# Seven block products in another order, with a third temporary for weight sums, and restored activations loaded behind the gate's weights

## The reference

```python
h = rms_norm(x, norm_g) * (1.0 + scale) + shift
u = h @ w_in          # (2048 x 1024) @ (1024 x D_IN)
(m_q, m_k, m_v, m_o, m_z, m_i, m_f, f_q, f_k, f_v, f_z, f_f) = jnp.split(u, SPLIT_IDX, axis=-1)
# m_q, m_k: causal conv of 4 taps + SiLU; f_q, f_k: RMS norm of each head
# m_v, m_o, f_v: values and an output gate, used as they are
# gate (of c @ w_ada) multiplies the layer's output at the very end
```

## Time and profile before

| | us |
|---|---|
| median of three runs | 1598.61 |
| the profiled execution | 1593.53 |
| its span | 1591.7 |
| PE busy in the span | 1471.6 (92%) |
| DVE busy | 997.8 (63%) |
| ACT busy | 645.1 (41%) |
| granted TensorE clock, mean | 0.974 |

### The profile page before, as it was taken

One profiled execution on the slowest core, in us unless ns is written; L12 is line 12 of the kernel. 1 busy time (PEld: TensorE's weight loads), 2 busy tenths in 40 slices (PEclk: granted clock), 3 DMA queues, 4 the chain that ended last, 5 costly groups with the idle time before them and its releaser, 6 DMA issues.

```text
span 1591.7 us, 21613 instructions
## 1 busy us (share of the span) xinstructions
PE 1471.6 (92%) x7673; PEld 1110.9 (70%) x7673; DVE 997.8 (63%) x2194; ACT 645.1 (41%) x1024; POOL 262.8 (17%) x370
## 2 busy tenths in 40 slices
PE   2999899999499998999999899999999997999998
PEld 2678777778388886887777665555555555888886
DVE  5867777762442466356678585766766747676774
ACT  4733544421021222344445566565655644222220
POOL 2034111102100000011111312103111000122221
PEclk8999999999799999999999999999999999999999
DMA  9374556559653422356665634223151047566761
GB/s 345 133 256 159 178 215 229 214 192 262 198 197 113 140 94 84 129 202 212 226 222 192 186 100 133 54 74 125 45 174 49 16 87 241 164 200 176 188 186 68
DMA packets 157291, 256.95 MB, mean 161 GB/s; under 512 B 11165, under 2 KB 94249, under 8 KB 155833
## 3 DMA queue, kind: packets, MB, share of 16 engines
q1 hardware_dynamic: 132304, 166.45, 34.6%
q0 software_dynamic: 24896, 89.31, 15.2%
HBM read 164.11 MB, written 91.62 MB: 161 GB/s over the span
## 4 chain that ended last, share of the span: by engine, by line
PE 61%; DVE 13%; DMA 12%; ACT 5%; issue 5%; SPq 3%; POOL 0%; DVEq 0%; ACTq 0%
PE a_ps_u L1333 13%; PE m_ps_out L2573 10%; PE f_ps_o L2108 8%; PE f_ps_t L2083 7%; DMA w_in_land<-in_w_in 7%; PE f_ps_s L2071 7%; PE a_ps_u L1290 5%; PE a_ps_u L1264 4%; DVE u_copy L956 2%; DMA gate_piece<-in_w_ada 1%; DMA a_ada_rows<-in_w_ada 1%; SPq L2404 1%; DVE u_copy L967 1%; DVE stage L927 1%; DVE gate_piece L982 1%
## 5 line engine op out<-in xcount | busy, mean ns | idle before, releaser
L1333 PE MATMUL a_ps_u<-v_hi,a_h_hi 128*128 128x512 f32 x384 | 152.5, 397 | 30.8 <-ACT stage L1698 18.7
L1333 PE MATMUL a_ps_u<-v_hi,a_h_lo 128*128 128x512 f32 x384 | 151.4, 394 | 0.0
L956 DVE TENSOR_TENSOR u_copy<-a_ps_u,u_copy 128x512 f32<-128x512 f32 x140 | 94.0, 686 | 27.0 <-PE a_ps_u L1290 24.7
L1333 PEld LDWEIGHTS a_ps_u<-v_hi,a_h_hi 128*128 128x128 f32 x384 | 73.6, 192 | 47.9 <-ACT stage L1698 19.1
L2243 ACT ACTIVATE f_probs_t<-f_ps_t 128x512 f32<-128x512 f32 (+1 forms) x128 | 65.3, 549 | 99.4 <-PE f_ps_t L2083 99.4
L1290 PE MATMUL a_ps_u<-a_h_hi,w_late 128*128 128x512 f32 x320 | 103.0, 389 | 0.0
L1290 PE MATMUL a_ps_u<-a_h_hi,w_in_lo 128*128 128x512 f32 x320 | 101.8, 389 | 0.0
L1290 PE MATMUL a_ps_u<-a_h_hi,w_in_hi 128*128 128x512 f32 x320 | 101.8, 389 | 0.0
L2573 PE MATMUL m_ps_out<-m_w_hi,w_in_hi 128*128 128x512 f32 x256 | 85.9, 412 | 2.0 <-DVE m_update L2726 2.0
L1698 ACT ACTIVATE stage<-a_ps_u 128x512 f32<-128x512 f32 x48 | 28.5, 601 | 142.6 <-PE a_ps_u L1333 128.7
L1333 PEld LDWEIGHTS a_ps_u<-v_hi,a_h_lo 128*128 128x128 f32 x384 | 73.5, 191 | 15.6
(11 more groups left out here) (388 smaller groups left out, 3554.5 us busy)
## 6 DMA issues: line engine op xcount, KB each, us to landing
w_in_land<-in_w_in SPq DMA_DIRECT2D x21, 1024.0 KB, 7.9
scratch_arrays<-stage POOLq DMA_DIRECT2D x14, 1024.0 KB, 4.9
scratch_arrays<-stage POOLq DMA_DIRECT2D x20, 512.0 KB, 3.1
w_in_land<-in_w_in SPq DMA_DIRECT2D x40, 256.0 KB, 3.4
scratch_kept<-w_in_lo POOLq DMA_DIRECT2D x18, 512.0 KB, 3.1
w_in_lo<-scratch_kept POOLq DMA_DIRECT2D x18, 512.0 KB, 3.9
scratch_qkT<-stage POOLq DMA_DIRECT2D x16, 512.0 KB, 4.0
scratch_qkT<-u_copy POOLq DMA_DIRECT2D x16, 512.0 KB, 6.9
```

Source lines behind the costliest of these rows:

```text
L956: dve.tensor_add(out, bank_of(s), other).then_inc(added_up, 1)
L1333: ins = pe.matmul(ps_u[:, half, c, :], h[:, k, first:first + P], w, start=(k == 0 and h is h_hi and w is not v_lo[k]), stop=(k == KT - 1 a ...
```

## The change

The change orders the seven products so that the three which read a block of the landed pair as it is come first, uses a third temporary (in the place of the gates' weights, which are done by then), loads a pair's weights when slot 2 and all four sums of the pair before are done, and orders DVE's, ACT's and POOL's work in a period to match. In the value stage the four restores move behind the gate's pieces and between value blocks, the store of unit 0 moves ahead of a wait in the gates' chain, and the last eight value blocks are split before the combinations. The diff is shown with most of its unchanged lines left out and twelve leading blanks removed.

```diff
@@ -120,6 +120,8 @@
 wg_land = lsb("wg_land", [P, KT, 2 * M_HEADS + F_HEADS])
+with nc.sbuf_tensor("a1_third_sum", [P, NB], F32) as third_sum:
+    pass
 w_gates = lsb("w_gates", [P, KT, GATE_ROWS], F32R)
@@ -278,7 +280,7 @@
 ADDS = 7
-KEPT = (1, 2, 3, 6)
+KEPT = (3, 4, 5, 6)
 KEPT_PAIRS = FIRST_PAIRS - 1
@@ -299,8 +301,8 @@
 
-    return [(LOWER, columns(w, 0)), (UPPER, columns(1 - w, 1)), (LOWER, columns(1 - w, 0)), (LOWER, columns(1 - w, 1)),
-            (UPPER, columns(w, 0)), (UPPER, columns(1 - w, 0)), (UPPER, columns(w, 1))][s]
+    return [(LOWER, columns(w, 0)), (UPPER, columns(w, 0)), (UPPER, columns(1 - w, 0)), (UPPER, columns(1 - w, 1)),
+            (LOWER, columns(1 - w, 0)), (LOWER, columns(1 - w, 1)), (UPPER, columns(w, 1))][s]
 
@@ -317,8 +319,9 @@
 sum_a, sum_b = (as_weights(stage[:, 1, WINDOW + i * NB:WINDOW + (i + 1) * NB]) for i in range(2))
-SLOT_SOURCE = [A11, sum_b, sum_a, sum_a, A12, A22, sum_b]
-SUMS_NEEDED = [0, 2, 1, 4, 0, 0, 3]
+sum_c = as_weights(third_sum[:, :])
+SLOT_SOURCE = [A11, A12, A22, sum_b, sum_a, sum_c, sum_b]
+SUMS_NEEDED = [0, 0, 0, 2, 1, 3, 4]
 
@@ -416,7 +419,6 @@
             eng.wait_ge(combined_lo, 4 * HALF_K)
-            eng.wait_ge(kept_moved[KEPT.index(s)], KEPT_PAIRS * 16)
         elif s < 6:
@@ -498,7 +500,8 @@
         elif p != FIRST_PAIRS:
-            sp.wait_ge(slot_lo, built_count(p - 1, 5))
+            sp.wait_ge(slot_lo, built_count(p - 1, 2))
+            sp.wait_ge(sums_ready, 4 * min(p, FIRST_PAIRS + 1))
         sp.dma_start(pair_land, w_view[:, :, bass.ds(tile_column(kind, i), 2 * P)]).then_inc(w_landed[0], 16)
@@ -507,8 +510,7 @@
                 sp.wait_ge(product_done, PRODUCTS * FIRST_PAIRS)
-                for s in (1, 3):
-                    sp.wait_ge(kept_moved[KEPT.index(s)], KEPT_PAIRS * 16)
+                sp.wait_ge(kept_moved[KEPT.index(3)], KEPT_PAIRS * 16)
             for f in range(2):
@@ -533,14 +535,17 @@
         load_pair(p)
-    sp.wait_ge(slot_lo, built_count(FIRST_PAIRS - 1, 5))
+    sp.wait_ge(slot_lo, built_count(FIRST_PAIRS - 1, 2))
+    sp.wait_ge(sums_ready, 4 * FIRST_PAIRS)
     load_values(0, KT + 4)
     sp.wait_ge(product_done, PRODUCTS * FIRST_PAIRS)
-    for b in (2, 3):
+
+    def restore(b, i):
         here = slice((b - 2) * NB, (b - 1) * NB)
         sp.wait_ge(later_moved, 4 * 16)
-        for i, h in enumerate((h_hi, h_lo)):
-            sp.dma_start(h[:, :, b * NB:(b + 1) * NB].bitcast(F32), scratch["later"][i, :, :, here]).then_inc(later_moved, 16)
+        h = (h_hi, h_lo)[i]
+        sp.dma_start(h[:, :, b * NB:(b + 1) * NB].bitcast(F32), scratch["later"][i, :, :, here]).then_inc(later_moved, 16)
+
     load_raw(1)
@@ -552,9 +557,14 @@
     load_raw(0)
-    load_values(20, 24)
+    restore(2, 0)
+    load_values(20, 22)
+    restore(2, 1)
+    load_values(22, 24)
     load_raw(2)
     load_raw(3)
+    restore(3, 0)
+    restore(3, 1)
     load_values(24, 28)
@@ -696,12 +706,12 @@
         if p + 1 < KEPT_PAIRS:
-            keep_slot(p + 1, 1)
-            keep_slot(p + 1, 2)
+            keep_slot(p + 1, 3)
         if p and p - 1 in WORKED:
...
         if p + 1 < KEPT_PAIRS:
-            keep_slot(p + 1, 3)
+            keep_slot(p + 1, 4)
+            keep_slot(p + 1, 5)
         if p and p - 1 in WORKED:
@@ -731,6 +741,7 @@
     pool.dma_start(f_ends[:, :], scratch["f_end"]).then_inc(chain_loaded, 16)
+    store_unit(0)
     wait_step(pool, "m_next_ready")
@@ -738,7 +749,6 @@
     pool.dma_start(neg_before[:, :], as_rows("f_before")).then_inc(chain_loaded, 16)
-    store_unit(0)
     wait_step(pool, "decay_ready")
@@ -915,15 +925,20 @@
                 elif p:
-                    dve.wait_ge(slot_lo, built_count(p - 1, 3))
+                    dve.wait_ge(slot_lo, built_count(p - 1, 4))
             elif i == 1:
...
                     dve.wait_ge(slot_lo, built_count(p - 1, 6))
+            elif i == 2:
+                if p:
+                    dve.wait_ge(slot_lo, built_count(p - 1, 5))
+                else:
+                    dve.wait_ge(gates_taken, TB)
             else:
-                dve.wait_ge(slot_lo, built_count(p, i - 1))
+                dve.wait_ge(slot_lo, built_count(p, 3))
             out, left, right, op = ((sum_a, A21, A22, ALU.add), (sum_b, sum_a, A11, ALU.subtract),
-                                    (sum_b, A12, sum_b, ALU.subtract), (sum_a, A11, A21, ALU.subtract))[i]
+                                    (sum_c, A11, A21, ALU.subtract), (sum_b, A12, sum_b, ALU.subtract))[i]
             dve.tensor_tensor(out=out, in0=left, in1=right, op=op).then_inc(sums_ready, 1)
@@ -941,17 +956,17 @@
 
-        s = [1, 3, 2, 2, 4, 5, 6][i]
-        out, other = [(u_block(p, 0, 1), u_block(p, 0, 0)), (u_block(p, 1, 0), u_block(p, 0, 1)),
-                      (u_block(p, 1, 1), u_block(p, 1, 0)), (u_block(p, 0, 1), u_block(p, 0, 1)),
-                      (u_block(p, 0, 0), u_block(p, 0, 0)), (u_block(p, 1, 0), u_block(p, 1, 0)),
+        s = [3, 1, 5, 4, 4, 2, 6][i]
+        out, other = [(u_block(p, 0, 1), u_block(p, 0, 0)), (u_block(p, 0, 0), u_block(p, 0, 0)),
+                      (u_block(p, 1, 0), u_block(p, 0, 1)), (u_block(p, 1, 1), u_block(p, 1, 0)),
+                      (u_block(p, 0, 1), u_block(p, 0, 1)), (u_block(p, 1, 0), u_block(p, 1, 0)),
                       (u_block(p, 0, 1), u_block(p, 0, 1))][i]
...
             dve.wait_ge(x_taken, p + 1)
-        elif i != 4:
-            dve.wait_ge(added_up, ADDS * p + [0, 1, 2, 1, 0, 3, 4][i])
-        if i == 1:
+        else:
+            dve.wait_ge(added_up, ADDS * p + [0, 1, 1, 3, 3, 4, 5][i])
+        if i == 2:
             wait_u(dve, p, 1)
@@ -1043,38 +1058,35 @@
             first_step(prev, turns(prev)[0])
-        add_up(p, 0)
         if build is not None:
-            sums(build, (0, 1))
+            sums(build, (0, 1, 2))
             low_slot(build, 0)
             low_slot(build, 1)
-            sums(build, (2,))
         if worked:
             first_step(prev, turns(prev)[1])
-        for i in (1, 2, 3):
-            add_up(p, i)
+        if build is not None:
+            low_slot(build, 2)
+        add_up(p, 0)
+        add_up(p, 1)
         if worked:
...
         if build is not None:
-            low_slot(build, 2)
+            low_slot(build, 3)
             sums(build, (3,))
-        add_up(p, 4)
+        elif p == FIRST_PAIRS - 1:
+            for k in range(4):
+                split_value(k)
         if worked:
...
         if build is not None:
-            low_slot(build, 3)
-        elif p == FIRST_PAIRS - 1:
-            for k in range(4):
-                split_value(k)
-        add_up(p, 5)
+            low_slot(build, 4)
+        for i in (2, 3, 4, 5):
+            add_up(p, i)
+        if build is not None:
+            low_slot(build, 5)
         if worked:
             second_step(prev, turns(prev)[1])
-        if build is not None:
-            low_slot(build, 4)
-        if worked:
             third_step(prev, turns(prev)[1])
-        if build is not None:
-            low_slot(build, 5)
 
@@ -1162,16 +1174,14 @@
     low_combined(0, 2)
-    sums(0, (0, 1))
+    sums(0, (0, 1, 2))
     plain(2)
     low_combined(0, 3)
-    low_slot(0, 0)
-    low_slot(0, 1)
-    sums(0, (2,))
-    low_slot(0, 2)
+    for s in range(4):
+        low_slot(0, s)
     sums(0, (3,))
     plain(3)
-    for s in range(3, 6):
+    for s in (4, 5):
         low_slot(0, s)
@@ -1210,22 +1220,19 @@
         differences(k)
-    split_values(32, 36)
+    split_values(32, PIECES_OF_V)
     for k in (0, 1):
...
         differences(k)
-    split_values(36, PIECES_OF_V)
     for k in (2, 3):
         low_combined(1, k)
-    sums(FIRST_PAIRS, (0, 1))
-    low_slot(FIRST_PAIRS, 0)
-    low_slot(FIRST_PAIRS, 1)
-    sums(FIRST_PAIRS, (2,))
-    low_slot(FIRST_PAIRS, 2)
+    sums(FIRST_PAIRS, (0, 1, 2))
+    for s in range(4):
+        low_slot(FIRST_PAIRS, s)
     sums(FIRST_PAIRS, (3,))
-    for s in range(3, 6):
+    for s in (4, 5):
         low_slot(FIRST_PAIRS, s)
@@ -1274,16 +1281,16 @@
             pe.wait_ge(finished, {0: 3, 2: 4, 4: 2}[s])
-        if p == 0 and s == 1:
+        if p == 0 and s == 2:
             pe.wait_ge(combined_lo, 2 * HALF_K)
...
         elif s == 6:
-            pe.wait_ge(added_up, ADDS * p + 2)
+            pe.wait_ge(added_up, ADDS * p + 1)
         elif p:
-            pe.wait_ge(added_up, ADDS * (p - 1) + {1: 1, 2: 4, 3: 7, 4: 5, 5: 6}[s])
+            pe.wait_ge(added_up, ADDS * (p - 1) + {1: 2, 2: 6, 3: 7, 4: 5, 5: 3}[s])
         rows, cols = operand(w, s)
@@ -1517,7 +1524,7 @@
             return
-        if s in (0, 4, 5):
+        if s < 3:
             act.wait_ge(w_landed[0], (2 + p + 1) * 16)
@@ -1632,20 +1639,22 @@
             first_step(prev, second)
+        if build is not None:
+            high_slot(build, 2)
         if worked:
...
         if build is not None:
-            high_slot(build, 2)
+            high_slot(build, 3)
         if worked:
```

(8 more changed lines are left out.)

## The result

The changed kernel takes 1544.16 us, the median of four runs (1542.01 to 1544.65), against 1598.53 for the kernel before, run beside it. The ratio is 0.9655, with a 95% interval of 0.9638 to 0.9671: 54.4 us less. The forecast was 1542.8, range 1531 to 1562.

The account below looks back on a forecast made before the run. TensorE was taken as the bound. Gains of 12.1 (window one), 37.0 (value stage) and 6.7 (window two) sum to 55.8 us: profiled 1593.5 to 1537.7, plus 5.1 to the median, 1542.8 us; range 1531 to 1562.

Parts of the forecast that it names:

- The ceiling: Both windows and value stage: TensorE loses 70.2 us to waits and low clock, the most this change can gain.
- Window one: First window's block products: earlier loads end VectorE's waits but the first; 4.6 us lost in place of 16.7, gain 12.1.
- the 2.8 us wait: First period of window one: TensorE's wait before product 6 shrinks from 4.8 to 2.8 us, with 1.5 of low clock.
- The gain that it implied: Window one: at the skill page's 4.4 us per load the last wait would go, gain some 4 us larger.
- The value stage: Value stage between the windows: its waits go with their low clock, 37.0 of 37.8 us gained, 0.8 stays.
- the 18.7, 4.7 and 6.6 us: Value stage: TensorE's three old waits, two blamed on restores ahead of gate weights, one on late splits; all to go.
- at 5.2 us each: Value stage: seven gate sums follow the first, made at 17 us, at 5.2 us each, ending at 55.
- rival 1: Value stage: unit 2's store, beside queued restores, makes ScalarE late; 2 us wait, up to 2 of clock; 1545 to 1548; chance 0.15.
- Window two: Second window: three pairs lose about 1.9 us each in place of 4.3, last tile waits 3.2; net gain 6.7.
- Rival 2: Both windows: VectorE becomes the bound, squares 1.4 us late in every NORM pair, window two gains nothing; 1555; chance 0.15.
- Rival 3: Value stage: restores land too late for the second half of tokens, wanted at 125 us; slower, about 1605; chance 0.03.
- Rival 4: Window one: the load starts no earlier in effect, so the window gains only 2 us; 1553; chance 0.07.

Follow-up runs that it names:

- e1_order_only: The changed kernel with the value stage's three edits put back as in the kernel before, leaving the new product order alone: 1576.79 us, ratio 0.987.
- e3_restores_back: The changed kernel with the four restores again ahead of the gate's weights in SP's queue: value stage 288.4 us, 19.0 more than in the changed kernel.
- e4_store_back: The changed kernel with the store of unit 0 again behind the gates' chain on POOL: value stage 273.7 us, 4.3 more than in the changed kernel.
- e7_split16: The changed kernel with value column blocks 16 and 17 split before the first two convolutions: value stage 268.8 us, 0.6 less than in the changed kernel.

## Why the prediction was right, and where it was off

**The ceiling** held. Pace and count gave 197.7 us for a window and 261.2 for the value stage; 198.8 and 261.5 were reached, with TensorE busy throughout.

**Window one** was forecast at 12.1 and gave 16.4. The step that failed is the price of the load in the first period, taken as 10.3 us from the earlier trace rows. This is where that load landed:

```profile
153.20 0.69 DVE L942 TENSOR_TENSOR stage<-w_in_land 128x512 f32<-128x512 f32 x1 [2.70 <-DMA w_in_land<-in_w_in]
```

It was issued at 147.7, so it took 5.5 us, and the 2.8 us wait with its slow clock never came. The row with 10.3 was a load issued behind the stores of kept slots; the change issues it before them (POOL's begin at 149.5). `e6_load_late` has the same order of products with the load back among these stores (it is issued at 148.9, the first of them at 148.5), and there it takes 10.7 us:

```profile
159.59 0.69 DVE L942 TENSOR_TENSOR stage<-w_in_land 128x512 f32<-128x512 f32 x1 [10.16 <-DMA w_in_land<-in_w_in]
```

I had moved the load in time and kept the duration of its old neighbours. The lower of the two rows, 6.3, would have been right to within 1 us, and with it too the wait is gone: the addition before product 6 ended at 157.6 and was wanted at 160. The mechanism is shown by the late load: 15.4 of the 16.4 us return. Of the 4.3 us between forecast and gain, 0.8 are a border: the forecast ends window one at 356.6, the table at the first matmul of the value stage, 357.3; 0.7 of the value stage's miss is the same border. VectorE waited once more, 2.9 us, where the forecast had none: the next load was issued at 159.9 behind the store of a kept slot and took 10.6 us. That wait cost TensorE nothing. The estimate from the Trainium skill ("DMA: Bandwidth & Descriptors", Anatomy of one DMA), 4.4 us, is 1.1 below the measured 5.5; the page fits it to transfers that GpSimd issues, and this load is SP's. The gain that it implied, some 4 us larger, is what came.

**The value stage** was forecast at 37.0 and gave 28.9. The steps for the waits held: the 18.7, 4.7 and 6.6 us are gone, the gate sums start at 17 us, unit 0 is stored at 36.6, the restores meet no wait, and each edit undone brings waits back after the half steps where they stood, though of other lengths (after 16 and 19 for the restores, after 19 for the store, after 86 for the splits). The step that failed is "at 5.2 us each" for all seven further gate sums, with the last at 55 us: the second came 17.4 us after the first, and the last ended at 69. That brought the wait of 5.8 us and 2.0 us of slow clock behind it. The cause stood in the earlier trace rows, the store of 0.2 KB that took 14.8 us. I read it as a victim of the restores and made rival 1 of it; it was itself what held up the others, as the three kernels with other stores show. In the earlier trace rows the first sum waits until 403.96 behind restores and stores alike, so that trace could not tell them apart. With the column stores mended the stage gains 36.8, against the forecast's 37.0.

**Window two** was forecast at 6.7 and gave 5.3. VectorE is the bound there as argued: three pairs with 0.47 us before product 6 (forecast 0.15, from 16.5 against 16.35) and 1.2 before the head means (1.35), and 3.8 in place of 3.2 at the last tile. These sizes, not the path, are what was off:

```profile
687.49 0.47 PE L1297 MATMUL a_ps_u<-a_h_hi,k 128*128 128x512 f32 x1 [0.47 <-DVE u_copy L971]
...
697.10 0.50 PE L1310 MATMUL a_ps_u<-squares,a_head_mean 128*128 128x512 f32 x1 [1.21 <-DVE v_lo L976]
...
819.86 0.76 PE L1271 MATMUL a_ps_u<-a_h_hi,w_in_hi 128*128 128x512 f32 x1 [3.76 <-DVE w_in_lo L1243]
```

**The sum** was 55.8 us against a measured 49.6 in the profiled executions, so the profiled execution was forecast 6.2 us too low: 8.1 by the value stage, 1.4 by window two, 0.9 by the first and last stretch, less 4.3 by window one (rounded figures). The median came within 1.4 us only because the 5.1 us between the profiled execution and the median of before were added, and this is no property of the kernel: the changed kernel's profiled execution lies 0.2 us from its median. The two errors cancelled.

**The rivals.** Rival 1 did not come: no store beside the restores was waited for, and its row proved something else. Rival 2 did not come: in window one the squares keep their margin, and window two gained. Rival 3 did not come, but it was nearer than the forecast had it. The last restore was issued at 437.5 us and landed 25.9 us later, 121 us after the stage's start in place of 100. TensorE, some 8 us late by then, reached it at 133. Rival 4 is excluded by VectorE's 5.6 us. The mark named for rival 1, TensorE waiting for ScalarE's takes, is absent in the changed kernel; it appears in `e1_order_only` (17.6 us), `e3_restores_back` (5.8), `e4_store_back` (9.4) and `e7_split16` (5.1).

## What to carry to other kernels

When a step is moved, its duration does not move with it: ask which transfers stood beside it in the old place and which will in the new. A long row beside heavy traffic may be the cause of the delay and not its victim, so price the smallest transfer of the stretch by itself before blaming the largest. And where one engine's wait is mended and another of the same length appears, look for what is late for both; compare by stage, since untouched code alone moved the total by up to 6 us here, and repeat a stage before reading small differences in it.

## What the runs showed of the hardware

A store of one float32 from each of 64 or 128 partitions into neighbouring 4-byte places of DRAM is slow and holds up others: three such stores, 1 KB in all, took 14.7 us to land, and a load of 512 KB from another queue issued beside them took 16.6 us in place of 3.9. They landed one after another, at 365.6, 370.5 and 373.4 us, so some 0.06 us for each of the 256 values, an estimate from these times. With the values 64 or 512 bytes apart the last of the stores landed in 1.7 us, and whole rows of 32 KB, 128 times the bytes, in 1.8. That it is the placing of the values in DRAM is shown. Spreading them also made the three arrays larger and may have moved them; that the distance counts and not the address is argued, from two distances and the whole rows, which all mend it. Why neighbours hold one another up was not tried, nor distances between 4 and 64 bytes. The Trainium skill ("DMA: Bandwidth & Descriptors", Queues, rings and completion order) says that a DMA engine changes between queues only at the end of a packet. That alone does not give the load's delay here: the stores' packets are recorded as short (0.01 us each), and it is the load's own packets that take 0.97 us in place of 0.13. What holds them stays open.

Behind the wait of 5.8 us in the changed kernel's value stage the clock is low for a while. The granted clock is 1.00 from 400 to 424.2 us and 0.65 from 430 to 436 (stretch as above), a mean of its two levels, 1.2 and 2.4 GHz:

```profile
430.00:436.00 6.00, 5.90 (x18) 4.74 (x19) 4.16 (x8) 0.00 (x0) 0.63 (x1) 0.65 0.99 335
```

```profile
430.10 0.77 PE L1340 MATMUL a_ps_u<-v_hi,a_h_hi 128*128 128x512 f32 x1 [5.81 <-DVE v_lo L1119]
430.67 0.63 PE L1340 MATMUL a_ps_u<-v_lo,a_h_hi 128*128 128x512 f32 x1
431.09 0.63 PE L1340 MATMUL a_ps_u<-v_hi,a_h_lo 128*128 128x512 f32 x1
```

After a first step of 0.57 us come eight of 0.43, the half pace of the earlier trace rows, one of 0.28, and then 0.23 again: 2.0 us on top of the wait. The same follows the 3.8 us wait at the last tile, in six steps of 0.43 from 820.4 us.
